# Query tiles first, memory projections from raw weights, and norms applied behind the projection

## The reference, cut to what matters

```
h = rmsnorm(x) ; proj = h @ w_in             # q 512, k 64, v 64, qi 256, ki 64, wi 4, glu 1024 columns
q, k, qi, ki = partial_rope(...)             # cos/sin of position * frequency on 16 of 64 columns
score = sum_h wi_h * relu(qi_h . ki)         # causal; the 128 best keys of each query are kept
a_out = softmax(q . k, chosen keys only) @ v # 8 heads, blocks of 128 queries
u = ga * sigmoid(gg) ; u = causal_dwconv(u, 31 taps)      # 512 channels
b_out = silu(layernorm(u))
x = x + concat(a_out, b_out) @ w_out
```

```
y = concat(rms_norm(y_lru, norm_lru_out), rms_norm(y_att, norm_att_out))
x = x + y @ w_out_2
```

## Time and profile before

| | us |
|---|---|
| median of 3 runs | 1419.82 (1416.19 to 1422.59) |
| the profiled execution, its own time | 1419.84 |
| its span, first to last instruction | 1418.0 |
| TensorE's mean granted clock | 0.983 of full |
| busy: TensorE / VectorE / ScalarE / POOL | 1367.1 / 780.3 / 539.2 / 606.4 |

### The profile page before, as it was taken

The page is one execution under the profiler, slowest core; times in us unless marked ns, Lnnn a source line. Parts: engine busy times, 40 slices in busy tenths (PEclk is TensorE's granted clock), DMA queues, the critical chain, the costliest instruction groups (busy, mean ns, idle before and its releaser), DMA issues.

```text
span 1418.0 us, 18066 instructions
## 1 busy us (share of the span) xinstructions
PE 1367.1 (96%) x6240; PEld 1096.9 (77%) x6240; DVE 780.3 (55%) x1091; ACT 539.2 (38%) x843; POOL 606.4 (43%) x295
## 2 busy tenths in 40 slices
PE   7999898999999999999999999999999999999997
PEld 5687776887777888888888777666778888888885
DVE  6698995253446777777523588655453333332222
ACT  4454667253333232223223353534342322323321
POOL 3487981342134444444444433122244444444341
PEclk8999999999999999999999999999999999999998
DMA  6122320121122232223322222111123232223321
GB/s 220 45 90 82 112 75 31 60 89 60 60 74 90 92 101 92 101 95 114 102 87 91 89 75 74 45 45 45 45 89 100 92 100 92 103 94 103 101 91 71
DMA packets 31876, 121.20 MB, mean 85 GB/s; under 512 B 3536, under 2 KB 3664, under 8 KB 31568
## 3 DMA queue, kind: packets, MB, share of 16 engines
q1 hardware_dynamic: 31392, 119.55, 25.0%
q10 hardware_dynamic: 432, 0.96, 0.3%
HBM read 118.40 MB, written 2.10 MB: 85 GB/s over the span
## 4 chain that ended last, share of the span: by engine, by line
PE 74%; issue 13%; POOL 5%; DVE 4%; ACT 2%; DMA 1%; POOLq 0%; SPq 0%; DVEq 0%; ACTq 0%
PE acc L1615 60%; POOL weights_low L584 3%; PE acc L1753 3%; POOL conv L633 2%; PE aux L1985 1%; PE aux L2005 1%; PE acc L1725 1%; PE aux L1987 1%; DVE aux L1154 1%; PE aux L1839 1%; PE aux L1820 1%; DVE a_low L1310 1%; DMA weights_raw<-w 1%; PE aux L1809 1%; PE aux L1995 1%
## 5 line engine op out<-in xcount | busy, mean ns | idle before, releaser
L584 POOL TENSOR_TENSOR weights_low<-weights_raw,weights_high 128x1024 fp32r<-128x1024 f32 (+1 forms) x204 | 524.6, 2572 | 781.9 <-ACT weights_high L661 778.9
L661 ACT CAST weights_high<-weights_raw 128x1024 fp32r<-128x1024 f32 (+1 forms) x202 | 221.8, 1098 | 511.3 <-PE acc L1615 478.8
L1615 PE MATMUL acc<-a_high,weights_high 128*128 128x512 f32 x976 | 390.0, 400 | 4.5 <-POOL weights_low L584 3.1
L1615 PE MATMUL acc<-a_high,weights_low 128*128 128x512 f32 x976 | 381.2, 391 | 0.0
L1615 PE MATMUL acc<-a_low,weights_high 128*128 128x512 f32 x976 | 380.8, 390 | 0.0
L1615 PEld LDWEIGHTS acc<-a_high,weights_high 128*128 128x128 f32 x976 | 183.9, 188 | 47.0 <-issue 6.3
L1615 PEld LDWEIGHTS acc<-a_low,weights_high 128*128 128x128 f32 x976 | 184.0, 189 | 39.5 <-issue 2.6
L1615 PEld LDWEIGHTS acc<-a_high,weights_low 128*128 128x128 f32 x976 | 183.8, 188 | 38.9
L1127 DVE TENSOR_TENSOR residual<-acc,residual 128x512 f32<-128x512 f32 (+1 forms) x64 | 44.0, 687 | 197.4 <-PE acc L1615 140.0
L1615 PE MATMUL acc<-h_high,weights_high 128*128 128x512 f32 x352 | 137.6, 391 | 0.0
L1615 PE MATMUL acc<-h_high,weights_low 128*128 128x512 f32 x352 | 137.0, 389 | 0.0
(11 more groups left out here) (347 smaller groups left out, 1920.2 us busy)
## 6 DMA issues: line engine op xcount, KB each, us to landing
weights_raw<-w SPq DMA_DIRECT2D x172, 512.0 KB, 3.2
weights_raw<-w SPq DMA_DIRECT2D x32, 704.0 KB, 4.0
residual<-xT SPq DMA_DIRECT2D x8, 256.0 KB, 7.2
out<-y_tok SPq DMA_DIRECT2D x4, 512.0 KB, 3.7
mem_raw<-memT SPq DMA_DIRECT2D x1, 1024.0 KB, 5.4
mem_tok<-mem SPq DMA_DIRECT2D x1, 1024.0 KB, 7.4
lru_weights<-blockdiag ACTq DMA_DIRECT2D x1, 512.0 KB, 3.4
sine<-positions ACTq DMA_DIRECT2D x1, 256.0 KB, 7.0
```

The lines of the kernel that those rows point to most:

```text
L584: g.tensor_tensor(weights_low[:, s, 0:cols], weights_raw[:, s, 0:cols], weights_high[:, s, 0:cols].bitcast(F32), ALU.subtract).then_inc(we ...
L661: a.copy(weights_high[:, s, 0:cols], weights_raw[:, s, 0:cols]).then_inc(weight_high, 1)
L1615: last = t_.matmul(acc[:, bank, 0:cols], w[:, s, wide], x_[:, k0 + k, 0:cols], start=start and k == opens and n == 0, stop=stop and k == c ...
```

## The change

In the first layer:

- The tiles of `w_in` come in a new order: key+wi, index queries, key/value, the first glu pair, then the four query tiles, then the other three glu pairs. Tiles 10 to 15 (the three pairs) with their `gate` and `glu` items are among the attention's first eight steps. 12 of the 16 `best` rounds are in these eight steps too, and the mask (`chosen`) is placed at the end of step 7 (queries of block 0 need only the causal mask).
- `first_tiles` finishes tile 0 before tile 1's low passes. ScalarE does the high parts of x first, and makes the split of chunk 2 as soon as tile 0 is done.
- The memory projections are one float32 matmul each, from `weights_raw` and `m_raw`: no high and low parts of 16 chunks and of the memory. The transfer of these chunks waits for `chunk_done`, the end of the chunk two before.
- The gain on the memory moves from POOL to ScalarE. `glu_scale` is gone: VectorE multiplies a glu tile with the factor as it leaves the accumulator (`glu_out`), in the place of ScalarE's copy.
- The convolution: VectorE 52 taps, ScalarE and POOL 72 products (69 additions).
- Angles are in `aux[4]`, the squares' sum in `aux[5]` (PSUM). The positions are loaded by SP behind x. `mem_root` is earlier, `mean` one step earlier, `ln_spread` and `ln_low` one step earlier, `second` starts one step later.

In the second layer the high and low parts of `y_lru` and `y_att` are made without the norm factor, with the gain alone, `y_att`'s as each block is finished; the factor is copied into a row (`lru_row`, `att_row`) and VectorE multiplies each result tile in the accumulator with it ahead of the addition to the residual (`normed_residual`), for all 16 tiles.

The diff, cut to its core:

```diff
-        SHARED_TAPS = 9
-        PRODUCTS = [(1, k) for k in range(SHARED_TAPS)] + [(0, k) for k in range(TAPS)]
-        CONV = [(n, k) for n in (2, 3) for k in range(TAPS)] + [(1, k) for k in range(SHARED_TAPS, TAPS)]
+        SHARED_TAPS = 10
+        PRODUCTS = ([(0, k) for k in range(TAPS)] + [(2, k) for k in range(SHARED_TAPS)]
+                    + [(3, k) for k in range(TAPS)])
+        CONV = [(1, k) for k in range(TAPS)] + [(2, k) for k in range(SHARED_TAPS, TAPS)]
+        GLU = (4, 5, 10, 11, 12, 13, 14, 15)
+        FIRST_PLAN = [("tile", 0, 0, KB), ("tile", 1, 0, KB), ("tile", 2, 0, KB), ("sum",), ("key_turn", 0),
+                      ("query_turn", 0), ("tile", 3, 0, 2), ("spread",), ("mem_root",), ("key", 0), ("query", 0),
+                      ("tile", 3, 2, KB), ("query_turn", 1), ("wi",), ("query", 1), ("tile", 4, 0, 4)]
+        FIRST_PLAN += [("causal",), ("tile", 6, 0, 4), ("glu_out", 1), ("key_turn", 1), ("best",), ("gate", 0),
+                       ("tile", 6, 4, KB), ("glu", 0), ("key", 1), ("query_turn", 2), ("best",), ("query", 2),
+                       ("v",), ("tile", 7, 0, 4), ("mem_scale", 0, 4), ("tile", 7, 4, KB), ("query_turn", 3),
...
+        FILLS = [("tile", n, 4 * half, 4 * half + 4) for n in range(10, 16) for half in range(2)]
+        FILLS += [("fill", n, 4 * half, 4 * half + 4) for n in range(2 * KB) for half in range(2)]
+        BEST_AT = (2, 1, 2, 1, 2, 1, 2, 1)
+        FIRST_TAP, LAST_TAP, FIRST_PRODUCT, LAST_PRODUCT, EARLY = 8, 23, 0, 22, 7
+            if step < len(BEST_AT):
+                FIRST_PLAN += [("best",)] * BEST_AT[step]
+            if step in (2, 4, 7):
+                FIRST_PLAN += [("gate", (step + 1) // 2 - (step == 7)), ("glu", (step + 1) // 2 - (step == 7))]
+                elif what == "glu_out":
+                    b, s = j // 2, j % 2
+                    dve.wait_ge(chunk_done, GLU[j] + 1)
+                    v.tensor_tensor(gate[:, b] if s else glu[:, b, TAPS - 1:TAPS - 1 + T], acc[:, s],
+                                    row_factor[:], ALU.mult).then_inc(tile_out[s], 1)
...
+                    for i in range(k, end):
+                        last = t_.matmul(acc[:, n % 2, 0:MB * P], weights_raw[:, q % 2, i * P:(i + 1) * P],
+                                         m_raw[:, i], start=i == 0, stop=i == KB - 1)
+                for b in range(MB):
+                    last = t_.matmul(acc[:, b], m_raw[:, 2 * part + i, b * P:(b + 1) * P],
+                                     weights_raw[:, q % 2, i * T:(i + 1) * T], start=part == 0 and i == 0,
+                                     stop=part == 3 and i == 1)
...
+        REC_PLAN += [("att_square", 3), ("last", 0, 0), ("last", 1, 0), ("att_sum",), ("last", 0, 1),
+                     ("last", 1, 1), ("att_spread",), ("last", 0, 2), ("last", 1, 2), ("att_row",)]
+            def normed_residual(s, n, t, row):
+                own.then(v.tensor_tensor(acc[:, s], acc[:, s], row, ALU.mult))
+                add_residual(s, n, t)
```

More of the change, by code:

```diff
@@ L363, in build @@
+        IN_INDEX = [("tile", 4, 4, 6), ("tile", 4, 6, KB)] + [("tile", 5, 2 * k, 2 * k + 2) for k in range(4)]
         for n in range(len(INDEX)):
[L364 to L377, removed]
@@ L388, in build, with share @@
-        CONV_STEPS, PRODUCT_STEPS = 25, 24
+        FILLS_AT = (1, 2, 2, 2, 2, 2, 2, 2, 1, 2, 1, 1, 1, 2, 1, 1, 1, 1, 1, 2, 1, 1, 1, 1, 1, 1, 1, 1, 2, 1, 1, 1)
+        BEST_AT = (2, 1, 2, 1, 2, 1, 2, 1)
+        FIRST_TAP, LAST_TAP, FIRST_PRODUCT, LAST_PRODUCT, EARLY = 8, 23, 0, 22, 7
+        def share(count, step, first, last):
+            steps = last - first + 1
+            at = min(max(step - first, 0), steps)
+            return range(at * count // steps, min(at + (step >= first), steps) * count // steps)
@@ L389, in build @@
         for step in range(len(DSA) + 3):
             fills = FILLS_AT[step] if step < len(DSA) else 0
+            now, FILLS = FILLS[:fills], FILLS[fills:]
             if step < len(DSA):
                 FIRST_PLAN.append(("logits", step))
[L393 to L394 removed]
+            for n, item in enumerate(now):
+                if n == (fills + 1) // 2 and 2 <= step < len(DSA) + 2:
+                    FIRST_PLAN.append(("prob", step - 2))
+                FIRST_PLAN.append(item)
+                if item[0] == "tile" and item[1] > 10 and item[3] == 4 or item[:3] == ("fill", 0, 0):
+                    FIRST_PLAN.append(("glu_out", GLU.index(item[1] - 1 if item[0] == "tile" else 15)))
@@ L407, in build @@
+            if step == 7:
+                FIRST_PLAN.append(("chosen",))
+            FIRST_PLAN += [("tap", i) for i in share(len(CONV), step, FIRST_TAP, LAST_TAP)]
+            FIRST_PLAN += [("product", EARLY + i)
+                           for i in share(len(PRODUCTS) - EARLY, step, FIRST_PRODUCT, LAST_PRODUCT)]
             if step >= 10 and step % A_HEADS == 2:
@@ L593, in low_after @@
             def low_after(q):
-                low((q + 2) // 2, q % 2, KB * P)
+                if not CHUNK["kc"] <= q + 2 < CHUNK["out"]:
+                    low((q + 2) // 2, q % 2, KB * P, splits(q + 2))
             low(0, 0, KB * P)
@@ L739, in _ @@
                 j = n[0] if n else 0
-                if what == "tile" and n[2] == KB:
+                if what == "tile" and n[2] == KB and j >= 2:
                     tile_ends(j)
@@ L1694, in in_tile @@
+                for k in range(KB):
+                    last = part(1, k, 2)
+                last.then_inc(chunk_done, 1)
             def in_tile(n, k, end):
```

349 lines of the change are left out of this document (172 added, 177 removed).

## The result

The changed kernel takes 1429.18 us (median of 5, 1427.58 to 1433.4), the kernel before 1419.82 in the same session: 1.008 times as long, 95% interval 1.0059 to 1.0102 (the two medians alone give 1.0066). By the medians it is slower by 9.4 us, where 1408 was forecast. The profiled execution (1429.2, span 1427.4) stands for the median.

A forecast was written before the change was run, and what follows sets the result against it. TensorE is busy 96% of the span, but VectorE and POOL bound the first layer's attention in turn. 1419.84 - 12.9 (first layer) + 1.2 (second layer's output projection) = 1408.1 us; range 1398 to 1422.

The forecast's parts named there:

- The steps: Attention steps 0 to 24, first logits to `mean`: 104.5 us, with VectorE 99.5, TensorE 96.4, POOL 95 of work.
- I take 5%: Steps 0 to 24: loss added to VectorE's 99.5 us for engines waiting in order for each other, giving 104.5.
- upper bound of 115.5: Steps 0 to 24: VectorE's 99.5 us plus 16, if each of 25 steps loses 0.65.
- some 84 us of VectorE work ... 96%: Kernel before, first attention step to `mean`: VectorE's work in the 87.3 us, the other engines less full.
- The transfers: Chunk loads waiting for the chunk two before to be used up: 0 us, 1 us if the cover goes.
- The start: Up to tile 2: POOL ends at about 25.9, 2.7 us gained, and no half speed, 2.7 more.
- The query turns: Before the first attention step: TensorE waits for ScalarE's split and copy at three turns, 1.6 us each, 4.8.
- The second layer's output projection: The 2.88 us stall and half speed go; last eight tiles take 3.69 us each instead of 2.95; net +1.2.
- Packed: Rival: priced waits in the steps, query turns and silu stretch are hidden (5.0 + 4.8 + 2.5 less), 1396; chance 0.13.
- Opening steps locked at `glu_out`: Rival, steps 0 to 7: VectorE's `best` rounds delay the `glu_out` that frees TensorE's bank, +9, 1417; chance 0.16.
- Clock: Rival, steps and up to `second`: TensorE's mean clock falls to 0.8, 168 us instead of 145, +23, 1431; chance 0.11.
- Half speed in the last half: Rival, output projection's second half: TensorE at 1.2 GHz needs 5.5 us per tile, +12, 1420; chance 0.07.

The follow-up runs named there:

- e1: Changed kernel with the third conv block's ten shared taps given back to VectorE (60 additions on POOL instead of 69): 1421.7 us.
- e2: Changed kernel with five of the ten shared taps given back to VectorE (64 additions, 57 taps): 1427.4 us.
- e3: Changed kernel with 30 of the fourth conv block's 31 products and additions left out, not moved: 1419.5 us.
- e4: Changed kernel with ScalarE's high parts of the output projection's first two chunks behind the last `vc` and probabilities copies, not ahead: 1427.8 us.
- e5: Kernel before with only the memory projections taken from raw weights as float32 matmuls, with their loads as in the changed kernel: 1414.7 us.
- e6: Changed kernel with gated pairs 1 to 3 done together at step 7, two table loads in the steps instead of six: 1430.4 us.
- e10: Kernel before with raw memory projections and the second layer's norm applied behind its output projection: 1412.8 us.
- e17: Changed kernel with only query turns 2 to 4 moved half a tile later: 1426.5 us.
- e13: e7 with query turns 2 to 4 moved half a tile later: 1411.5 us.
- e14: Old tile order, raw memory projections, changed start, second layer's norm behind, 14 shared taps; tile 2 and two blocks of tile 3 before square sums' dependents: 1408.7 us.
- e7: Changed kernel with the edits of e1 and e4 and the memory's root moved behind the index stage: 1420.2 us.

## Why the prediction was wrong, step by step

1. **The steps, 104.5 forecast, 116.1 measured: the step that failed most.** VectorE's and POOL's sums were right to 5%. What failed is the overlap, "Three engines within 5% of each other can't all be full" and "I take 5%": the loss was not 5 us but 16.6, 0.6 more than the upper bound of 115.5. Two readings led there. First, "some 84 us of VectorE work ... 96%" for the kernel before is not what its trace shows:

```profile
131.10:218.40 87.30, 75.43 (x457) 63.90 (x455) 80.69 (x160) 57.26 (x124) 73.59 (x46) 0.94 0.27 91
```

VectorE was busy 80.7 of 87.3, 92%, so that stretch already lost 8%; the same loss on 99.5 would have given 108. Second, an addition was priced at its busy time. The additions are one chain through one buffer, and a link takes 1.42 us. At that, 64 additions are 91 us, and with five splits (12.0) and three gated products (3.3) POOL comes to 106, the fullest engine (my estimate from these rows). The 10 us left are of the kind of POOL's waits for ScalarE: 7.0 for high parts, 6.3 for products, 2.5 for gates. ScalarE feeds the chain through two product buffers and stands in order between it and TensorE, so POOL's lateness became ScalarE's, and TensorE's. e1, e2 and e3 show that the additions with their products set the stretch (7.8, 5.1 and 10.6 us). That POOL's half of the pair is the slow one rests on the waits, not on a run of its own. TensorE's own sum was 5 short as well (busy 101 to 102.5 for 96.4).
2. **The transfers, "I count 0 (1 us if that cover goes)".** Wrong by about 4 us (5.5 in e4's profile), with what follows behind `second`. I asked what hides the transfer from TensorE; it was ScalarE that waited, with TensorE's copies behind. That is more than half of the +5.9 and +2.1 of these stages. In the old order the same rule for the transfers cost 0.5 at most (e5, 35.0 for 34.5).
3. **The start.** Tile 2 came at 22.2, not 25.9, at full clock. The first logits came 2.3 late, which is within the spread of that stage (96.4 to 102.6 us over e1 to e4 and e6). The gain at tile 2 is taken back at ropes and roots: the memory's squares on ScalarE (2.1 us) stand ahead of the first rope, for which VectorE waited 2.6, and TensorE stood 2.0 at the first index product. No run shows what the root alone costs. The query turns cost 5.1 us for 4.8 forecast. That price was right, and I should have read it as the price of the new order: where the tiles keep the old one it is 0.
4. **The second layer's output projection.** Mechanism right, size too high: 3.46 per tile for 3.69. Row factor 3 to 4 went 1.0 us down instead of 1.2 up, but it spreads from 248.0 to 251.4 over profiles with this edit, and e10 shows no gain to speak of.
5. **The rivals.** Packed: no. Opening steps locked at `glu_out`: TensorE waited 0.4 us there, no. Clock: it was 1.00 in the steps, no. The case that the Trainium skill has for it (TensorE: Matmul & The Clock Gate, A second HAM failure mode), a clock that swings between groups, isn't met by this row. Half speed in the last half: clock 1.00, no. Slower came by none of them but by a fifth: serial waits on engines that are not full. `mean` came at 215, later than the 212 that I had named as wrong, and it was neither of the two causes I had named for that, `glu_out` and the clock. The table loads are not the excess: e6 took four of six away and won nothing, though its late gates may have eaten a gain.
6. **What I didn't weigh at all** is each part by itself. The raw memory projections alone make the kernel before 5 us faster (e5), and the other parts then lose 14. The stages put 7.8 at the additions, 4 to 5.5 at the transfer and 4 to 6 at the turns. The medians of the single edits give back less (7.5 in e1, 1.4 in e4, 2.7 in e17, 11.6 in all), and all three together, with the root moved, give 17.7 (e13). So they don't simply add, and a part of e13's gain is the clock. With these mended, the changed kernel is at 1411.5 (e13); in the old order with the start's gain covered it is at 1408.7 (e14).

## What to carry to other kernels

Where several engines are evenly loaded, don't add a few per cent to the fullest: look for the serial chain, take its period from start to start rather than its busy time, and ask which engine stands in order between it and the bound. When a wait moves to another engine, price what is queued behind it there. And test a change of many parts one part at a time: here one part was a gain of 5 us that the others hid. Before a stage's gain is put down to an edit, hold the clock of that stage in both traces against each other.

## What the runs showed of the hardware

- A two-input in-place POOL addition of 128x512 is busy 1.28 us, and a chain of them runs mostly at 1.41 to 1.42 us from start to start in the changed kernel, 1.43 to 1.44 in the kernel before. With a weight split behind it, the next instruction began after 1.24.
- TensorE's clock alone made 191 unchanged matmuls of one stretch busy 42.1 us (0.92, e7) or 38.8 (1.00, e13).
- VectorE's in-place `cosine` step of the start takes 0.43 us, but 2.06 in e4, where it begins while POOL's weight split runs, and it ends 0.3 us behind the split's end:

```profile
18.00 2.42 POOL L601 TENSOR_TENSOR weights_low<-weights_raw,weights_high 128x1024 fp32r<-128x1024 f32 x1 [5.70 <-ACT weights_high L662]
...
18.65 2.06 DVE L1112 TENSOR_SCALAR cosine<-cosine 128x512 f32<-128x512 f32 x1
```

- The memory's float32 matmuls cost TensorE more at full clock than three fp32r passes, and yet TensorE's busy time up to `second` rose by only 0.6 us in e5 (228.0 to 228.6), while the clock was 0.96 instead of 0.93 up to there.
